# Hybrid RWKV / attention step on one core: norms by head in every row, attention queries left unnormalized

## The chip, the cores and the metric

The kernel runs on one core of one Trainium2 chip. The metric is the device time of one execution in microseconds (us); lower is better.

## The reference, cut to what matters

One layer over 1024 prompt tokens and 64 sample tokens, D = 1024, all in float32: RMS norm, one input projection, three token mixers in parallel (RWKV-7 with 8 heads of 64, sliding-window attention with 8 query and 2 key heads of 64, cross-attention with 4 heads of 128 into 256 memory tokens), gates, output projection, then a convolutional feed-forward part. The four norms by head are what the change touches:

```
kk = kk / max(sqrt(sum(kk * kk over 64)), 1e-12)                  # RWKV key, 8 heads
o = (o - mean) * rsqrt(var + GN_EPS) * ln_g + ln_b                # RWKV output, 8 heads
q = rms(q, swa_qn_g); k = rms(k, swa_kn_g)                        # window attention, 8 + 2 heads
qm = rms(qm, mem_qn_g)                                            # cross-attention, 4 heads
s = q.k * 64**-0.5 - slope * dist;  s = qm.mk * 128**-0.5         # scores, then softmax
```

## The kernel before, in words

Activations lie with channels on the 128 partitions and tokens along the free dimension. Tokens go in three groups g = 0, 1, 2 of T = 384, 384 and 320. For each group there is a `mix_block` (projections, mixers) and an `ffn_block`.

Every engine runs two threads, interleaved by one list written out ahead (`order`, used by `weave`). The *dense* thread is the projections: weights come in units of 128x512 by DMA (SP queue), ACT copies a unit to `w_hi` (L206), POOL subtracts to get `w_lo` (L215), PE makes 12 matmuls of it (L235 to L237). A ring of five units lets ACT and POOL run ahead of PE. An entry 0 of `order` is half a unit: six matmuls. A tile is two units; when it ends, DVE reads it out of one of two accumulators (L1560 for `pr` tiles with the token shift L1539 to L1551 behind it, L1567 for gates), and PE can't start the tile after next before that. The *chain* thread is the mixers; an entry 1 is one step of it on every engine. Each engine executes its queue strictly in order, so a chain instruction that waits also holds up the dense work behind it.

In `mix_block` the chain has four parts:

- `prep`, 14 steps, one behind each of the RWKV tiles 2 to 13, then two more with half a tile of dense work between them. Step 9 sums the squares of `kk`, steps 10 to 13 make the inverse root, step 13 ends with the operands ready (`rp_done`).
- `scan`, the chunks of 64 tokens, which begins with a wait for `rp_done`.
- `post`, 9 steps: mean, variance, inverse root, gain, bias, gate, split in `o_hi`, `o_lo`.
- `attn_prep`, 8 steps: squares of the nine tiles of `pa` (four of queries, one of keys, four of memory queries), sums, inverse root, product; then `attn`, items of 128 queries with scores, softmax, transposes, values.

After `prep` the steps are spread evenly over the 132 half units that are left: 101 steps in groups 0 and 1, 97 in group 2.

A norm by head was made "in rows": `to_rows` is a set of constant matrices that add the squares of every head into one row of a PSUM tile of T columns (one accumulating matmul for each tile of 128 channels), the inverse root is computed once on 128xT, and `from_rows` matrices copy each row back to the partitions of its head (one matmul a tile). The inverse root is Ln, then Exp on ACT (`rsqrt_act`), then a Newton step of three DVE instructions (`rsqrt`, L287, L289, L291). Each instruction waits for the one before.

Of the kernel before, what the change touches and what calls it, by code (L numbers as in the profile page):

```python
# [11 lines left out]
ALU = mybir.AluOpType  # L12
AX = mybir.AxisListType

P = 128
# [267 lines left out]

def rsqrt(dve, xs, t, y, sem, n):

    dve.wait_ge(sem, n + 2)
    dve.tensor_tensor(t, xs, y, ALU.mult).then_inc(sem, 1)  # L287
    dve.wait_ge(sem, n + 3)
    dve.scalar_tensor_tensor(t, t, -0.5, y, ALU.mult, ALU.mult).then_inc(sem, 1)  # L289
    dve.wait_ge(sem, n + 4)  # L290
    dve.scalar_tensor_tensor(y, t, 1.5, y, ALU.add, ALU.mult).then_inc(sem, 1)  # L291
# [8 lines left out]
def first_block(nc, c):  # L300
    a, T = c.a, GROUPS[0][1]
    with Phase(nc, "first") as f:
# [18 lines left out]
        def _(sp):  # L321
            def chain():
# [10 lines left out]
                for dst, src in ((c.ident, "ident"), (c.ones_head, "ones_head"), (c.lora, "lora"),  # L333
                                 (c.to_rows, "to_rows"), (c.from_rows, "from_rows")):
                    sp.dma_start(dst[...], a[src]).then_inc(c.consts_in, 16)
# [227 lines left out]
N_PREP, N_POST, N_ATTN_PREP = 14, 9, 8  # L563
# [4 lines left out]
def mix_block(nc, c, g):  # L568
# [18 lines left out]
    with Phase(nc, f"g{g}m") as f:  # L587
# [15 lines left out]
        def rooms(at):  # L603
# [12 lines left out]
        mask, xs, t, y = (give(TW) for _ in range(4))  # L616
# [16 lines left out]
        nsq, nxs, nt, ny = give(4, TW), give(TW), give(TW), give(TW)  # L633

        asq, axs, at_, ay = give(4, TW), give(TW), give(TW), give(TW)
# [16 lines left out]
            "mean centred squared var n_root spread post o_hi o_lo "  # L652
            "a_squared a_rows a_root a_spread a_done before cache "
# [16 lines left out]
        def _(pe):  # L670
            def keys():
# [11 lines left out]
                pe.wait_ge(c.consts_in, 16 * 5)  # L683
# [6 lines left out]
            def prep():  # L690
# [28 lines left out]
                yield  # L719
                yield  # L720
# [7 lines left out]
                pe.wait_ge(S["dstep"], 5)  # L728
                products(*((1 + m, c.ones_head[:, :], t3[:, m, 0:T]) for m in range(4)))
# [97 lines left out]
            def post():  # L827
# [7 lines left out]
                for m in range(4):  # L835
                    mm = pe.matmul(bank[4][:, 0:T], c.to_rows[:, m, :], nsq[:, m, 0:T], start=(m == 0), stop=(m == 3))
                mm.then_inc(S["var"], 1)
# [3 lines left out]
                pe.wait_ge(S["n_root"], ROOT)  # L841
                for m in range(4):
                    pe.wait_ge(S["centred"], 4)
                    pe.matmul(bank[m][:, 0:T], c.from_rows[:, m, :], ny[:, 0:T], start=True, stop=True).then_inc(S["spread"], 1)
# [3 lines left out]
                yield  # L848

            def attn_prep():  # L850
                yield
                for ns in (range(0, 4), range(4, 8), range(8, 9)):
                    for n in ns:
                        pe.wait_ge(S["a_squared"], n + 1)
                        pe.matmul(bank[5][:, 0:T], c.to_rows[:, n, :], asq[:, n % 4, 0:T], start=(n == 0),  # L855
                                  stop=(n == 8)).then_inc(S["a_rows"], 1)
                    yield
# [4 lines left out]
                for n in range(9):  # L862
                    if n >= 5:
                        pe.wait_ge(S["a_done"], n - 4)
# [1404 lines left out]
```

## Time and profile before

| | |
|---|---|
| median of 3 runs | 2249.27 us (2247.49 to 2250.12) |
| the profiled execution | 2246.76 us, its span 2244.9 us |
| PE busy | 2117.5 us, 94% of the span |
| DVE, ACT, POOL busy | 1121.6, 938.4, 1136.6 us |
| mean granted TensorE clock | 0.983 |

PE's busy time counts from the start of a matmul to its modelled end, and matmuls overlap; how long a row of them holds the engine is read from the starts. A float32 matmul shows as two records.

### The profile page before, as it was taken

To read this page: it belongs to the slowest core of one execution; us is meant where nothing else is said; L and a number is where in the kernel's file an instruction comes from. 1 tells how busy PE (TensorE), PEld (TensorE's weight loads), DVE (VectorE), ACT (ScalarE), POOL (GpSimd) and SP (SyncE) were. 2 spreads that over 40 slices of the span, in tenths; PEclk is the share of its full clock that TensorE was granted. 3 is DMA by queue.
4 is the path that set the end of the run, shared out by engine and by line. 5 is a ranking of instruction groups with operands and counts; after the bars stand their busy time and mean duration, and the time that the engine had idled before them with its cause. 6 is when DMAs were issued, how large, how long until landed. Compare 5 with 4: busy or idle time off the path is not lost. (4 is left out here: it accounts for less than half of the span.)

```text
span 2244.9 us, 42906 instructions
## 1 busy us (share of the span) xinstructions
PE 2117.5 (94%) x17042; PEld 1972.2 (88%) x17042; DVE 1121.6 (50%) x2048; ACT 938.4 (42%) x1888; POOL 1136.6 (51%) x933
## 2 busy tenths in 40 slices
PE   5989999899999998999998999999999989899998
PEld 4878887799999987888788999999889877799998
DVE  5673345455665237433554566632664255457740
ACT  4422335445444433232463444444432355355542
POOL 5543333365666654333334656665543333567775
PEclk8999999999999999999999999999999999999999
DMA  5421122363444433112225534444321333644453
GB/s 177 147 67 58 57 85 91 126 213 113 127 126 145 147 123 94 49 48 79 91 78 184 173 113 127 126 149 139 116 76 54 91 112 97 195 152 147 146 159 123
DMA packets 158150, 264.86 MB, mean 118 GB/s; under 512 B 20096, under 2 KB 53120, under 8 KB 157952
## 3 DMA queue, kind: packets, MB, share of 16 engines
q1 hardware_dynamic: 157376, 261.08, 37.2%
q8 instruction: 136, 2.23, 0.4%
q10 hardware_dynamic: 576, 1.05, 0.1%
q14 instruction: 62, 0.51, 0.1%
HBM read 242.60 MB, written 19.46 MB: 117 GB/s over the span
## 5 line engine op out<-in xcount | busy, mean ns | idle before, releaser
L215 POOL TENSOR_TENSOR k_w_lo<-k_raw,k_w_hi 128x512 fp32r<-128x512 f32 x832 | 1088.3, 1320 | 1016.7 <-ACT k_w_hi L206 972.6
L206 ACT ACTIVATE k_w_hi<-k_raw 128x512 fp32r<-128x512 f32 x832 | 500.0, 617 | 383.4 <-PE k_acc L237 129.3
L235 PE MATMUL k_acc<-k_x_hi,k_w_hi 128*128 128x384 f32 (+1 forms) x1152 | 416.6, 362 | 15.0 <-PEq L70 10.0
L237 PE MATMUL k_acc<-k_x_hi,k_w_lo 128*128 128x384 f32 (+1 forms) x1152 | 379.1, 329 | 0.0
L236 PE MATMUL k_acc<-k_x_lo,k_w_hi 128*128 128x384 f32 (+1 forms) x1152 | 378.6, 329 | 0.0
L235 PEld LDWEIGHTS k_acc<-k_x_hi,k_w_hi 128*128 128x128 f32 x1152 | 219.2, 190 | 54.3 <-issue 29.9
L236 PEld LDWEIGHTS k_acc<-k_x_lo,k_w_hi 128*128 128x128 f32 x1152 | 219.4, 190 | 5.6 <-issue 1.4
L237 PEld LDWEIGHTS k_acc<-k_x_hi,k_w_lo 128*128 128x128 f32 x1152 | 218.5, 190 | 0.0
L235 PE MATMUL k_acc<-k_o_hi,k_w_hi 128*128 128x384 f32 (+1 forms) x288 | 98.0, 340 | 24.4 <-POOL k_w_lo L215 9.7
L235 PE MATMUL k_acc<-g0f_xg_hi,k_w_hi 128*128 128x384 f32 x352 | 118.7, 337 | 2.2 <-DVE g0f_a_raw L1982 2.2
L235 PE MATMUL k_acc<-g1f_xg_hi,k_w_hi 128*128 128x384 f32 x352 | 118.7, 337 | 2.2 <-DVE g1f_a_raw L1982 2.2
L236 PE MATMUL k_acc<-g1f_xg_lo,k_w_hi 128*128 128x384 f32 x352 | 118.3, 336 | 0.0
L236 PE MATMUL k_acc<-g0f_xg_lo,k_w_hi 128*128 128x384 f32 x352 | 118.2, 336 | 0.0
L237 PE MATMUL k_acc<-g1f_xg_hi,k_w_lo 128*128 128x384 f32 x352 | 118.2, 336 | 0.0
L237 PE MATMUL k_acc<-g0f_xg_hi,k_w_lo 128*128 128x384 f32 x352 | 118.1, 336 | 0.0
L235 PE MATMUL k_acc<-g2f_xg_hi,k_w_hi 128*128 128x320 f32 x352 | 110.6, 314 | 2.4 <-DVE g2f_a_raw L1982 2.4
L236 PE MATMUL k_acc<-g2f_xg_lo,k_w_hi 128*128 128x320 f32 x352 | 109.4, 311 | 0.0
L237 PE MATMUL k_acc<-g2f_xg_hi,k_w_lo 128*128 128x320 f32 x352 | 109.4, 311 | 0.0
L236 PE MATMUL k_acc<-k_o_lo,k_w_hi 128*128 128x384 f32 (+1 forms) x288 | 96.5, 335 | 0.0
L237 PE MATMUL k_acc<-k_o_hi,k_w_lo 128*128 128x384 f32 (+1 forms) x288 | 96.3, 335 | 0.0
L235 PEld LDWEIGHTS k_acc<-k_o_hi,k_w_hi 128*128 128x128 f32 x288 | 55.7, 193 | 30.0 <-POOL k_w_lo L215 20.3
L737 PEld LDWEIGHTS g0m_bank<-g0m_room 64*64 64x64 f32 x1728 | 64.7, 134 | 10.1 <-issue 9.1
(710 smaller groups left out, 4476.6 us busy)
## 6 DMA issues: line engine op xcount, KB each, us to landing
k_raw<-w_up SPq DMA_DIRECT2D x264, 256.0 KB, 2.8
k_raw<-w_gate SPq DMA_DIRECT2D x144, 256.0 KB, 3.1
k_raw<-w_down SPq DMA_DIRECT2D x96, 256.0 KB, 3.8
k_raw<-w_rwkv SPq DMA_DIRECT2D x84, 256.0 KB, 3.0
k_raw<-w_branch SPq DMA_DIRECT2D x72, 256.0 KB, 3.5
k_raw<-w_attn SPq DMA_DIRECT2D x60, 256.0 KB, 2.9
k_raw<-w_out SPq DMA_DIRECT2D x48, 256.0 KB, 3.0
k_raw<-w_down_end SPq DMA_DIRECT2D x24, 256.0 KB, 3.4
```

Of the source, the lines that this page charges most:

```text
L206: act.activation(c.w_hi[s][:, 0:n], c.raw[s][:, 0:n], ACT.Copy).then_inc(c.hi_done, 1)
L215: pool.tensor_tensor(c.w_lo[s][:, 0:n], c.raw[s][:, 0:n], c.w_hi[s][:, 0:n].bitcast(F32), ALU.subtract).then_inc(c.lo_done, 1)
L235: pe.matmul(out, wh, xh, start=(u.begins and k == 0), stop=False)
L236: pe.matmul(out, wh, xl, start=False, stop=False)
L237: mm = pe.matmul(out, wl, xh, start=False, stop=(u.ends and k == u.kt - 1))
L737: mm = pe.matmul(out[h, j, :], lhs[h, j, :], rhs[h, j, :], start=(k == 0), stop=(k == len(operands) - 1))
```

## The change

1. `prep`: the four `to_rows` matmuls of step 9 become four with `ones_head` (a matrix that adds over the 64 partitions of a head and gives the sum to all of them), each into a bank of its own. DVE reads four banks. The inverse root is made on 128x4T; the Newton instructions go to step 11 (one) and 12 (two). The four `from_rows` matmuls go; one DVE product over 128x4T takes the place of four from PSUM. The bonus sums (four matmuls) move from step 13 to step 11. `B` is computed last.
2. `post`: the same, with 11 steps; the Newton instructions, 128x4T each, stand in steps 6, 7 and 8, gain and bias together in step 9.
3. `attn_prep`: nine squares into nine tiles. One matmul for the keys' sums (128xT), then eight with 32 columns of `ones_head` or `ones` into the four quarters of the partitions of two banks: the sums of the query heads. ACT copies these, PE turns them (two transposes an item), DVE reads 12 numbers for each query, and ACT and DVE make inverse roots `qf` of 128x36. The nine `from_rows` matmuls and eight of the nine products are gone. The keys are normalized as before and multiplied by the query gain on ACT into `kq`.
4. `attn`: `qf` stands in place of the constant 0.125 where the scores are read (four instructions of 256 columns a step for two of 512) and as the scale of the memory's Exp. The memory keys are multiplied by `mqn` once (`c.mk` in group 0, `cmk` in group 2).
5. 1.2 MB less of constants are loaded; the mix phase has four semaphores more (six new, two gone).

```diff
@@ prep, PE
-                pe.wait_ge(S["tan"], 2 + 7)
+                pe.wait_ge(S["tan"], 2 + 8)
+                pe.wait_ge(S["g_done"], 2)
                 pe.wait_ge(S["sq_done"], 1)
                 for m in range(4):
-                    mm = pe.matmul(bank[0][:, 0:T], c.to_rows[:, m, :], sq[:, m, 0:T], start=(m == 0), stop=(m == 3))
-                mm.then_inc(S["rows"], 1)
-                yield
-                yield
-                yield
-                pe.wait_ge(S["p_root"], ROOT)
-                pe.wait_ge(S["g_done"], 4)
-                products(*((b, c.from_rows[:, m, :], y[:, 0:T]) for m, b in ((0, 5), (1, 0))))
-                yield
-                pe.wait_ge(S["got"], 2)
-                products(*((b, c.from_rows[:, m, :], y[:, 0:T]) for m, b in ((2, 5), (3, 0))))
-                pe.wait_ge(S["tan"], 10)
+                    pe.matmul(bank[m][:, 0:T], c.ones_head[:, :], sq[:, m, 0:T], start=True, stop=True).then_inc(S["rows"], 1)
+                yield
+                yield
+                pe.wait_ge(S["p_root"], 1)
                 pe.wait_ge(S["dstep"], 5)
-                products(*((1 + m, c.ones_head[:, :], t3[:, m, 0:T]) for m in range(4)))
+                products(*((m, c.ones_head[:, :], t3[:, m, 0:T]) for m in range(4)))
@@ prep, DVE
+                for m in range(4):
+                    dve.wait_ge(S["rows"], m + 1)
+                    ins = dve.tensor_scalar(xs[:, m, 0:T], bank[m][:, 0:T], 1e-24, None, ALU.max)
+                ins.then_inc(S["p_root"], 1)
+                yield
+                yield
+                root = (xs[:, :, 0:T], t[:, :, 0:T], y[:, :, 0:T], S["p_root"], 1)
+                newton(dve, 0, *root)
+                yield
+                newton(dve, 1, *root)
+                newton(dve, 2, *root)
+                yield
+                dve.wait_ge(S["p_root"], ROOT)
+                dve.tensor_tensor(ar[:, X_KK, 0:T], ar[:, X_KK, 0:T], y[:, :, 0:T], ALU.mult).then_inc(S["got"], 1)
+                dve.wait_ge(S["mixed"], 14)
+                for m in range(4):
+                    dve.wait_ge(S["prod"], 12 + m + 1)
+                    dve.tensor_tensor(ar[:, X_BONUS.start + m, 0:T], bank[m][:, 0:T], ar[:, X_V.start + m, 0:T], ALU.mult)
+                dve.wait_ge(S["got"], 1)
+                dve.tensor_tensor(ar[:, X_B, 0:T], ar[:, X_KK, 0:T], t2[:, :, 0:T], ALU.mult).then_inc(S["rp_done"], 1)
@@ post, DVE
+                for k in range(3):
+                    yield
+                    newton(dve, k, nxs[:, :, 0:T], nt[:, :, 0:T], ny[:, :, 0:T], S["n_root"], 1)
+                yield
+                dve.wait_ge(S["n_root"], ROOT)
+                for m in range(4):
+                    dve.scalar_tensor_tensor(o[:, m, 0:T], o[:, m, 0:T], vec(c, "ln_g", m), ny[:, m, 0:T], ALU.mult,
                                              ALU.mult).then_inc(S["post"], 1)
@@ attn_prep, PE
+                pe.wait_ge(S["a_squared"], 9)
+                pe.matmul(bank[5][:, 0:T], c.ones_head[:, :], asq[:, 4, 0:T], start=True, stop=True).then_inc(S["a_rows"], 1)
+                pe.wait_ge(S["n_root"], 1)
+                for j in range(4):
+                    rows = slice(32 * j, 32 * j + 32)
+                    pe.matmul(bank[4][rows, 0:T], c.ones_head[:, 0:P:4], asq[:, j, 0:T], start=True, stop=True)
+                for j in range(4):
+                    rows = slice(32 * j, 32 * j + 32)
+                    mm = pe.matmul(bank[0][rows, 0:T], c.ones[:, 0:32], asq[:, 5 + j, 0:T], start=True, stop=True)
+                mm.then_inc(S["q_rows"], 1)
+                yield
+                yield
+                pe.wait_ge(S["q_read"], 1)
+                for n, b in enumerate((4, 0)):
+                    for p, it in enumerate(items):
+                        mm = pe.transpose(bank[b][0:it.nq, p * P:(p + 1) * P], q_rows[:, n, it.q0:it.q0 + it.nq], c.ident[:, :])
+                mm.then_inc(S["q_turned"], 1)
@@ attn, ACT
+                act.activation(kq[:, k_all], kw[:, k_all], ACT.Identity, scale=vec(c, "qn")).then_inc(S["kq"], 1)
@@ attn, DVE
+                    for jj in range(2):
+                        i, col = 4 * e + 2 * half + jj, 2 * (2 * half + jj) + e
+                        ins = dve.scalar_tensor_tensor(
+                            s[p % 2][0:it.nq, i, 0:nk], bank[2 * half + e][0:it.nq, jj * 256:jj * 256 + nk],
+                            qf[0:it.nq, p, col:col + 1], c.alibi[0:it.nq, i, it.first:2 * P], ALU.mult, ALU.add)
```

## Rows read from the trace of the kernel before

**Rows 1.** The page, busy time of each engine

```profile
PE 2117.5 (94%) x17042; PEld 1972.2 (88%) x17042; DVE 1121.6 (50%) x2048; ACT 938.4 (42%) x1888; POOL 1136.6 (51%) x933
```

**Rows 2.** Waits of PE over the span: us in total, times, longest

```profile
PE g2m_bank L688 <- DVE g2m_room L291: 4.9, 1, 4.9
PE g1m_bank L688 <- DVE g1m_room L291: 4.4, 1, 4.4
...
PE g1m_bank L865 <- DVE g1m_room L291: 2.6, 1, 2.6
```

**Rows 3.** Timeline of PE, end of `prep` in group 1: start, us, instruction

```profile
872.64 2.82 PE L716 MATMUL g1m_bank<-g1m_room,k_to_rows 128*128 128x384 f32 x8 [2.79 <-ACT g1m_room L998]
881.15 0.41 PE L235 MATMUL k_acc<-k_x_hi,k_w_hi 128*128 128x384 f32 x1 [1.53 <-DVE g1m_ar L1560]
894.15 2.93 PE L688 MATMUL g1m_bank<-g1m_room,k_from_rows 128*128 128x384 f32 x4 [4.41 <-DVE g1m_room L291]
908.43 1.92 PE L737 MATMUL g1m_bank<-g1m_room 64*64 64x128 f32 x32
```

**Rows 4.** Timeline of DVE, the same stretch

```profile
882.30 0.55 DVE L1234 TENSOR_SCALAR g1m_room<-g1m_bank 128x384 f32<-128x384 f32 x1
...
886.21 1.43 DVE L1539 TENSOR_TENSOR g1m_ar<-g1m_ar 128x383 f32<-128x383 f32 x1
...
890.36 1.61 DVE L287 TENSOR_TENSOR g1m_room<-g1m_room 128x384 f32<-128x384 f32 x1
...
901.92 1.76 DVE L1247 TENSOR_TENSOR g1m_ar<-g1m_ar,g1m_room 128x1536 f32<-128x1536 f32 x1
903.60 1.94 DVE L1250 TENSOR_TENSOR g1m_ar<-g1m_bank,g1m_ar 128x384 f32<-128x384 f32 x4
```

**Rows 5.** Timeline of POOL, the same stretch

```profile
884.66 8.43 POOL L215 TENSOR_TENSOR k_w_lo<-k_raw,k_w_hi 128x512 fp32r<-128x512 f32 x6 [4.54 <-ACT k_w_hi L206]
900.74 1.27 POOL L215 TENSOR_TENSOR k_w_lo<-k_raw,k_w_hi 128x512 fp32r<-128x512 f32 x1 [7.64 <-ACT k_w_hi L206]
```

**Rows 6.** Timeline of ACT, the same stretch

```profile
871.01 1.48 ACT L998 ACTIVATE g1m_room<-g1m_ar 128x1536 f32<-128x1536 f32 x1 [7.94 <-DVE g1m_ar L1218]
...
882.88 0.53 ACT L278 ACTIVATE g1m_room<-g1m_room 128x384 f32<-128x384 f32 x1 [7.01 <-DVE g1m_room L1234]
```

**Rows 7.** A stretch of 4 us, columns as its head says

```profile
core 0: us, PE busy (x) PEld busy (x) DVE busy (x) ACT busy (x) POOL busy (x), PEclk, DMA share, GB/s
894.00:898.00 4.00, 3.85 (x8) 2.64 (x9) 2.90 (x8) 0.00 (x0) 0.00 (x0) 0.50 0.22 66
```

**Rows 8.** Groups of PE instructions by shape, group 1: busy, mean ns

```profile
L929 PE MATMUL g1m_bank<-k_ident,g1m_room 128*128 128x128 f32 x24 | 3.1, 272 | 0.0
```

**Rows 9.** Timeline of PE, `post` to `attn` in group 1

```profile
1066.60 2.74 PE L831 MATMUL g1m_bank<-g1m_o,k_ones_head 128*128 128x384 f32 x8
...
1115.87 1.13 PE L878 MATMUL g1m_bank<-g1m_kw,g1m_pa 64*128 64x256 f32 x8
...
1130.53 3.54 PE L921 MATMUL g1m_bank<-k_ident,g1m_room 128*128 128x128 f32 x16 [1.99 <-DVE g1m_room L1469]
...
1142.76 1.94 PE L942 MATMUL g1m_bank<-g1m_room 128*64 128x512 f32 x8
```

**Rows 10.** Timeline of DVE, `post` in group 1

```profile
1084.14 3.23 DVE L1379 SCALAR_TENSOR_TENSOR g1m_o<-g1m_o,k_vecs,g1m_ar 128x384 f32<-128x384 f32 x4
...
1117.05 1.29 DVE L1432 SCALAR_TENSOR_TENSOR g1m_room<-g1m_bank,k_alibi 128x512 f32<-128x512 f32 x2 [0.52 <-PE g1m_bank L878]
```

**Rows 11.** Timeline of ACT, last steps of `post`, last square of `attn_prep`, group 1

```profile
1087.87 1.93 ACT L1077 ACTIVATE k_o_hi<-g1m_o 128x384 fp32r<-128x384 f32 x4 [2.56 <-DVE g1m_o L1384]
...
1094.84 0.52 ACT L1085 ACTIVATE g1m_room<-g1m_pa 128x384 f32<-128x384 f32 x1 [0.28 <-PE g1m_bank L855]
```

**Rows 12.** Timeline of POOL where group 0's mix phase ends

```profile
446.16 1.26 POOL L215 TENSOR_TENSOR k_w_lo<-k_raw,k_w_hi 128x512 fp32r<-128x512 f32 x1 [9.38 <-issue]
```

More of the change, by code:

```diff
@@ L332, in chain @@
                 yield
-                for dst, src in ((c.ident, "ident"), (c.ones_head, "ones_head"), (c.lora, "lora"),
-                                 (c.to_rows, "to_rows"), (c.from_rows, "from_rows")):
+                for dst, src in ((c.ident, "ident"), (c.ones_head, "ones_head"), (c.lora, "lora")):
                     sp.dma_start(dst[...], a[src]).then_inc(c.consts_in, 16)
@@ L615, in mix_block @@
         t1, t2, t3, sq = (give(4, TW) for _ in range(4))
-        mask, xs, t, y = (give(TW) for _ in range(4))
+        mask, xs = give(TW), give(4, TW)
+        t, y = sq, t1
         half, one_ka = give(8), give(4)
@@ L632, in mix_block @@
         give = rooms(0)
-        nsq, nxs, nt, ny = give(4, TW), give(TW), give(TW), give(TW)
-        asq, axs, at_, ay = give(4, TW), give(TW), give(TW), give(TW)
+        nsq, nxs, ny = give(4, TW), ar[:, X_R, :], ar[:, X_V, :]
+        nt = nsq
+        give = rooms(0)
+        asq, axs, at_, ay = give(9, TW), give(TW), give(TW), give(TW)
+        q_rows = asq[:, 0:2, :]
+        kq = give(5 * P)
+        qxs, qt, qf = (give(3, 12) for _ in range(3))
         s = [give(8, 2 * P)]
@@ L651, in mix_block @@
             "t2 t2_read t3 t3_read s0p xs xs_read sa sa_read ssum state osum o_read "
-            "mean centred squared var n_root spread post o_hi o_lo "
-            "a_squared a_rows a_root a_spread a_done before cache "
+            "mean centred squared var n_root post o_hi o_lo "
+            "a_squared a_rows a_root q_rows q_read q_turned q_root a_done kq gained before cache "
             "v_turned v_tok scores biased topped sunk shifted exps summed inverse scaled turned pt_read pv "
@@ L835, in post, with attn_prep @@
                 for m in range(4):
-                    mm = pe.matmul(bank[4][:, 0:T], c.to_rows[:, m, :], nsq[:, m, 0:T], start=(m == 0), stop=(m == 3))
-                mm.then_inc(S["var"], 1)
+                    pe.matmul(bank[m][:, 0:T], c.ones_head[:, :], nsq[:, m, 0:T], start=True, stop=True).then_inc(S["var"], 1)
+                for _ in range(9):
+                    yield
+            def attn_prep():
                 yield
@@ L847, in post @@
                 yield
-                yield
-            def attn_prep():
-                yield
[L852 to L856, printed above, removed]
-                    yield
-                yield
-                yield
-                pe.wait_ge(S["a_root"], ROOT)
-                pe.wait_ge(S["post"], 4)
-                for n in range(9):
-                    if n >= 5:
-                        pe.wait_ge(S["a_done"], n - 4)
-                    pe.matmul(bank[n % 5][:, 0:T], c.from_rows[:, n, :], ay[:, 0:T], start=True,
-                              stop=True).then_inc(S["a_spread"], 1)
-                    if n in (4, 8):
-                        yield
             def scores(p, half):
@@ L884, in m_scores @@
                 keys = c.mk if it.own else cmk
+                if g == 0 and p == 0 or not it.own:
+                    pe.wait_ge(S["gained"], 1)
                 if p >= 1:
@@ L1071, in post @@
                 yield
-                rsqrt_act(act, c, nxs[:, 0:T], nt[:, 0:T], ny[:, 0:T], S["n_root"], 1)
-                for _ in range(5):
+                rsqrt_act(act, c, nxs[:, :, 0:T], nt[:, :, 0:T], ny[:, :, 0:T], S["n_root"], 1)
+                for _ in range(7):
                     yield
@@ L1082, in attn_prep @@
                 for n in range(9):
[L1083 to L1085 removed]
+                    act.activation(asq[:, n, 0:T], pa[:, n, 0:T], ACT.Square).then_inc(S["a_squared"], 1)
                     if n in (3, 7):
@@ L1109, in m_exps @@
                     ins = act.activation(pm[0:it.nq, h, :], bank[4 + h // 2][0:it.nq, (h % 2) * 256:(h % 2 + 1) * 256],
-                                         ACT.Exp, bias=mneg[0:it.nq, h:h + 1], scale=float(P) ** -0.5,
+                                         ACT.Exp, bias=mneg[0:it.nq, h:h + 1], scale=qf[0:it.nq, p, 8 + h:9 + h],
                                          accum_out=mtotal[0:it.nq, h:h + 1])
```

136 lines of the change are left out of this document (68 added, 68 removed).

## The prediction, made before the changed kernel was run

> **What bounds the kernel now.** I read the page first: PE is busy 94% of the span, the others about half of it [rows 1]. So PE's work is the time, plus the places where its queue stands still. The list of PE's waits comes next. The long ones inside a mix phase are the norms: the `from_rows` matmuls wait 4.4 and 4.9 us in `prep` and 2.6 us in `attn_prep` for the last Newton instruction [rows 2]. Then the timelines of one group, to see why, since PE runs a fixed order and a chain step that is late stops the dense work too. Group 1's `prep` shows it: PE stands 2.79 us before L716, 1.53 us for an accumulator that DVE hasn't emptied, and 4.41 us before `from_rows` at 894.15 [rows 3]. In those 4.41 us DVE wasn't idle. A 383-column product took 1.43 us and the first Newton instruction, 384 columns, 1.61 us [rows 4], while POOL made six `w_lo` in one piece, 8.43 us from 884.66 [rows 5]. An uncontended DVE instruction over 1536 columns takes 1.76 us, 0.46 us for 384 [rows 4]. So a DVE instruction with two SBUF inputs waits about 1.1 us for POOL's while POOL has a backlog.
>
> The Trainium skill has a rule for this (SBUF — State Buffer, "SBUF: two separate sides"): DVE with two SBUF inputs and GpSimd take one shared port pair in turns, exclusively, for a whole instruction. The trace agrees, 1.43 and 1.61 us for instructions of about 0.5 [rows 4].
>
> **Part 1, PE's work.** Four 384-column matmuls hold PE some 2.6 us (2.74 us less the tail under the next [rows 9]), 0.65 each. A group loses 17 `from_rows` matmuls, and eight of its `to_rows` matmuls become narrow ones: 25 x 0.65 = 16.2 us. The narrow ones have 32 columns each in quarters of their own. The trace has halves: four 512-column matmuls of 64 columns took 1.94 us [rows 9], where 0.65 x 512 / 384 x 4 is 3.5, so two run at once. Eight quarters cost 1.3 us (four at once) to 5.2 us (none), I take 2.0, between four and two at once. Six transposes, 0.26 us each (12 in 3.1 us [rows 8]): 1.6 us. Net -12.6 us, for T = 320 about -10.4: **-35.6 us** in all. This arrives only if PE doesn't stand longer.
>
> The Trainium skill (TensorEngine Tiling, "Tiling Modes") says that four 128x32 tiles work in parallel and that a change of tiling drains the engine. By that alone the eight cost 1.3 us plus a drain, and the sum would be about 2 us lower over the three groups. No row here shows quarters.
>
> **Part 2, prep.** What decides is when DVE has `rp_done`, because the scan waits for it. In group 1, on before's clock:
> - Nothing changes up to 882.30, where DVE now reads four banks, 1.9 us instead of 0.5 (L1234 and L1250 give 0.55 and 1.94 for four [rows 4]): done 884.2.
> - Ln and Exp over 1536 take 1.4 to 1.5 us each (the Square over 1536 took 1.48 [rows 6]): done 887.2, where before, at 0.53 each from 882.88 [rows 6], they were over by 884.0. ACT holds its weight units so long, and POOL's backlog starts at about 887.9 instead of 884.66 [rows 5].
> - PE: tile 12 from 881.15, 8 half units in the 8.59 us to 889.74 [rows 3], so 1.05 each; bonus sums at 885.4 (2.6 us); tile 13 until 892.1; then six half units until 898.4, and it is at the scan.
> - DVE: tile 13 read and shifted (1.9 us), from 892.4; Newton 2 and 3, product, `B`: four at 1.7; bonus four in 1.94 [rows 4]. Together 10.6: 903.0 if POOL never interferes. POOL has five units to make after 892.2 (six in one piece and one later [rows 5], now all after 887.9). If each costs DVE 1.1 us: 908. I take 907, since the timeline shows strict alternation under a backlog.
> - From `rp_done` to the first gram matmul lie ACT's decays and five DVE instructions. Before, `rp_done` was 905.5 (end of L1250 [rows 4]) and the gram's matmuls began at 908.43 [rows 3], with 0.5 us to spare: 2.4 us. After: 909.4, against 908.43. So the 5.2 us of PE work and the 4.41 us wait are gone, and one wait of 8.6 to 11 us at the scan has come: **+1.0 us** (bounds -3.1 to +2.2).
> - The clock. After the 4.41 us wait the granted clock was 0.50 over 894 to 898 [rows 7], the lower level, 1.2 GHz, while PE worked. That price is inside before's 908.43. The new wait puts as long a stretch behind the gram, inside the scan: some 4 us at half rate, **+2.0 us** (0 to 3).
>
> Sum for `prep`: +3.0 us a group.
>
> **Part 3, post and attn_prep.** Step k after `prep` stands behind half unit 132k/103, rounded up, instead of 132k/101 (in groups 0 and 1). `post`, step 52, so comes behind half unit 67 instead of 68: on group 1's clock before, 1065.55 instead of 1066.60 [rows 9]. Variance sums end 1073.8, the four reads by DVE 1074.6, Ln and Exp 1077.5. From there DVE is full: three Newton instructions 5.0, a gate tile 0.5, gain, bias and gate 12 x 0.52 = 6.3: 11.8 us. Five POOL units fall into it; before, one cost the four bias instructions 1.1 us (3.23 instead of 2.1 [rows 10]). With 4.5 us for them the gates end at 1094 (1089.5 to 1095). Before, `o_hi`, one behind each gate product, ended at 1089.8 [rows 11], now 1094.5. Behind `o_hi` on ACT lie nine squares, two weight units and a gate's Tanh: before 5.6 us (1094.84 + 0.52 [rows 11]), after 5.2, as they no longer wait for sums: 1099.7. DVE has then also left the gate tile of half unit 80 unread, so PE stands at half unit 84 from 1088.4 on, for 5 us, then 5 us more in step 4 of `attn_prep`. Sums 0.65 + 2.0: 1102.3. Three half units and 1.7 us for a stretch at half clock: 1107.1. Transposes 1.6, five half units 5.2, values' transposes 0.5: first scores at 1114.4. `kq` is ready for it: `qf`, then DVE's nine small or 384-wide instructions and ACT's `kq` end about 4.5 us behind the transposes, PE comes 5.7 behind. Before, 1115.87 [rows 9]: -1.5 us. From there on, latency rules until L921, where PE waits 1.99 us for DVE at the same half unit as before, so the half unit in hand is given back in that wait. The score reads cost 4 x 0.34 instead of 1.29 [rows 10], +0.1 us each. Sum: **-1.3 us** a group (bounds -5.9, without POOL's interference, and +4.0, with quarters that don't overlap and `kq` 2 us late).
>
> **Part 4, small ones.** POOL stands 9.38 us at the end of a mix phase [rows 12] while it clears its 106 semaphores, 0.09 each; four more are 0.35 us, and PE waits there for the next `w_lo`: +1.0 us in three. The gain on `c.mk`, `cmk` (under 1 us on DVE) lies in PE's waits. The constants: 0, as nobody waits for them.
>
> **Sum.** 3 x (3.0 - 1.3) + 1.0 = +6, less 1 because groups at T = 320 have shorter instructions: +5 on the profiled execution's 2246.76, 2251.8. The runs' median is 2.5 us above that execution: **2254 us**. So the 35.6 us of PE work come back as waits of DVE's longer row, plus clock.
>
> **Rivals.**
> - *A, POOL and DVE don't meet much.* If ACT's delay lets POOL fill the ring in PE's waits, DVE's lists go uncontended: -3.1 + 2.0 in `prep`, -5.9 behind, +1: 3 x -7.0 + 1 = -20, 2229 us. For it: POOL works only half the time [rows 1]. Against: it met DVE in every such stretch [rows 4, 5].
> - *B, the waits go and nothing takes their place.* -35.6 and some 25 us of waits at the norms (4.4 and 2.6 [rows 2] and their like): 2190 us. It needs DVE to be ready 9 us earlier than my list; only speaks for it that PE is the bound [rows 1].
> - *C, worse: quarters don't overlap,* 5.2 instead of 2.0, 3.2 us in each group directly in the row from squares to scores, +10: 2264 us; with POOL's full price in both lists 2270. Decides from 4 us for eight.
> - *D, half of A:* 2241 us.
>
> **How the numbers follow.** Forecast, with its own range of 2249 to 2259: 0.48; A 0.14; B 0.04; C 0.16; D 0.18. Predicted 2254 us. The range reaches from A to C's end, 2228 to 2270, and leaves out B and some of the edges. A measurement tells about 0.2%, 4.5 us. Faster: A, B and D, 0.36. Slower: C and half of the forecast, 0.40. The same: the other half, 0.24.
>
> **What would show it.** In the changed profile: no PE wait before `from_rows`, but one of 8 to 11 us at the head of the scan, with Newton instructions of 1.7 to 2.9 us on DVE; a low granted clock just behind it; a wait for DVE's gate tile and for ACT's squares before the first sums of `attn_prep`; eight narrow matmuls in about 2 us; first scores 50 us behind `post`. If DVE's wide Newton instructions come at 1.7 us each, or PE arrives at the scan with `rp_done` there, the forecast is wrong and A or B holds.

## The result, and the profile after

The changed kernel takes 2267.52 us (median of 4 runs, 2266.26 to 2271.13), the kernel before 2249.69 in the same comparison (2247.49 to 2251.02): a ratio of 1.0080, 95% interval 1.0066 to 1.0094. The prediction was 2254 in a range of 2228 to 2270. The profiled execution took 2266.89 us, 20.1 more than the one of before, where the sum of the steps said 5.

The page of the changed kernel, busy time of each engine, to be held against [rows 1]:

```profile
PE 2097.0 (93%) x16958; PEld 1959.9 (87%) x16958; DVE 1157.7 (51%) x2089; ACT 955.3 (42%) x1903; POOL 1153.0 (51%) x933
```

PE has 84 matmul records less and 20.5 us less to do, and not the 35.6 that were taken from it: its mean granted clock fell from 0.983 to 0.968. There are two levels, 1 and 0.5 of full speed, so the share of the span at 0.5 is 2 x (1 - the mean): some 76 us before and 145 now.

Where the time went is read best from the starts of five matmuls in each group: the first one of `prep`, the first of the gram, of `post`'s means and of the scores, and the last one of the memory values in `attn`. The last stage ends at the first own matmul of the ffn phase. Sums over the three groups, in us, difference to before (222.5, 448.2, 144.6, 227.7, 290.2), with all kernels that were run:

```
                 prep>gram  gram>post  post>scores  scores>values  values>ffn    sum
changed            +5.4       +6.7        -2.1         +12.3          -2.2      +20.1
forecast           +3.0       +2.9        -1.4          +0.6           0         +5
only_prep          +5.2       +5.9        +1.8          -1.8          -0.8      +10.3
only_post          -0.3       -1.0       +24.4          +5.6          +0.4      +29.1
only_attn          +1.1       -0.1       -14.8          +5.0          +2.2       -6.6
filler             +5.4       +5.7        -1.0         +10.0          -2.1      +18.0
light_pool         -8.8       +5.2        -9.8          +8.7          +0.3       -4.4
no_newton          -7.6       +4.2       -10.4          +8.4          +1.6       -3.8
plain_scores       +5.8       +5.8        -0.8          +6.5          +0.8      +18.1
both              -17.9       +3.3       -15.3         +10.1          +1.9      -17.9
attn_bonus         -6.0       +3.2       -11.8          +4.9          -1.4      -11.1
attn_nn            -9.6       +3.3       -17.0          +3.5          -1.6      -21.4
only_attn again    +0.5        0.0       -10.7          +4.5          -2.7       -8.4
attn_bonus again   -7.1       +1.7       -13.4          +5.3          -1.1      -14.6
```

Each row is one execution, read to 0.1 us. Two kernels have a second profile (the last two rows), and the same kernel differs from itself by up to 4.1 and 4.9 us in one stage, so a difference of a few us in one stage alone is not to be read as the kernel's.

The waits of PE in the changed kernel (us in total, times, longest), in place of [rows 2]:

```profile
PE g1m_bank L750 <- DVE g1m_ar L1274: 8.2, 1, 8.2
...
PE k_acc L235 <- DVE g1m_gt L1611: 5.2, 1, 5.2
...
PE g1m_bank L851 <- ACT g1m_room L1092: 2.9, 1, 2.9
```

No wait stands before a `from_rows` matmul any more. In its place stand 8.2 us at the head of the scan (L750) and, behind `post`, 5.2 us for a gate tile and 2.9 for the squares; the other groups have the same within 1.1 us. Now group 1's `prep`, the timeline of PE, as [rows 3]:

```profile
881.06 2.82 PE L728 MATMUL g1m_bank<-g1m_room,k_ones_head 128*128 128x384 f32 x8 [2.80 <-ACT g1m_room L1007]
...
889.58 0.41 PE L235 MATMUL k_acc<-k_x_hi,k_w_hi 128*128 128x384 f32 x1 [1.53 <-DVE g1m_ar L1604]
...
916.04 1.12 PE L750 MATMUL g1m_bank<-k_ident,g1m_ar 64*64 64x64 f32 x16 [8.22 <-DVE g1m_ar L1274]
918.43 1.97 PE L743 MATMUL g1m_bank<-g1m_room 64*64 64x128 f32 x16 [1.27 <-DVE g1m_room L1311]
```

and what DVE did in it, as [rows 4]:

```profile
896.27 1.75 DVE L288 TENSOR_TENSOR g1m_room<-g1m_room 128x1536 f32<-128x1536 f32 x1
...
906.04 2.84 DVE L290 SCALAR_TENSOR_TENSOR g1m_room<-g1m_room 128x1536 f32<-128x1536 f32 x1
908.91 1.76 DVE L292 SCALAR_TENSOR_TENSOR g1m_room<-g1m_room 128x1536 f32<-128x1536 f32 x1
...
914.24 1.75 DVE L1274 TENSOR_TENSOR g1m_ar<-g1m_ar,g1m_room 128x1536 f32<-128x1536 f32 x1
```

with POOL in one piece beside it, as [rows 5]:

```profile
896.40 10.86 POOL L215 TENSOR_TENSOR k_w_lo<-k_raw,k_w_hi 128x512 fp32r<-128x512 f32 x7 [7.85 <-ACT k_w_hi L206]
```

Read together: ACT's long Ln and Exp move POOL's backlog behind them, to 896.40 to 907.26. The second Newton instruction lies in it and takes 2.84 us, the third and the products lie behind it and take 1.75 each. PE has nothing to do for the 8.22 us before 916.04. What follows is read from windows (columns as the head says):

```profile
core 0: us, PE busy (x) PEld busy (x) DVE busy (x) ACT busy (x) POOL busy (x), PEclk, DMA share, GB/s
907.00:911.00 4.00, 0.82 (x5) 0.50 (x3) 3.93 (x3) 0.00 (x0) 0.26 (x1) 0.99 0.42 127
911.00:925.00 14.00, 7.69 (x73) 6.74 (x74) 10.47 (x23) 2.12 (x6) 2.12 (x4) 0.52 0.00 1
925.00:939.00 14.00, 13.57 (x240) 12.08 (x238) 5.25 (x14) 4.15 (x9) 5.56 (x7) 1.00 0.19 57
```

PE's last work before the wait ends at 907.8. By 911 the clock is at its lower level, where it stays for nearly 14 us, and PE works in some 7.2 of them (7.69 in the window, which ends a little later). In groups 0 and 2 the low stretches at this place are 13.7 and 10.2 us long, with PE at work in 7.1 and 5.1.

The same for `post` to `attn` of group 1, PE as in [rows 9]:

```profile
1079.05 2.74 PE L837 MATMUL g1m_bank<-g1m_o,k_ones_head 128*128 128x384 f32 x8
...
1107.27 0.66 PE L235 MATMUL k_acc<-k_x_hi,k_w_hi 128*128 128x384 f32 x1 [5.17 <-DVE g1m_gt L1611]
...
1112.43 1.65 PE L851 MATMUL g1m_bank<-g1m_room,k_ones_head 128*128 128x384 f32 x2 [2.90 <-ACT g1m_room L1092]
1114.01 1.51 PE L856 MATMUL g1m_bank<-g1m_room,k_ones_head 128*32 128x384 f32 x8
1115.30 1.01 PE L859 MATMUL g1m_bank<-g1m_room,k_ones 128*32 128x384 f32 x8
...
1127.93 1.14 PE L880 MATMUL g1m_bank<-g1m_room,g1m_pa 64*128 64x256 f32 x8 [1.98 <-ACT g1m_room L1135]
...
1130.94 2.01 PE L880 MATMUL g1m_bank<-g1m_room,g1m_pa 64*128 64x256 f32 x8
...
1145.60 2.95 PE L930 MATMUL g1m_bank<-k_ident,g1m_room 128*128 128x128 f32 x16 [4.46 <-DVE g1m_room L1509]
```

and DVE:

```profile
1091.19 1.76 DVE L288 TENSOR_TENSOR g1m_room<-g1m_ar 128x1536 f32<-128x1536 f32 x1 [0.97 <-ACT g1m_ar L280]
1092.98 2.74 DVE L290 SCALAR_TENSOR_TENSOR g1m_room<-g1m_room,g1m_ar 128x1536 f32<-128x1536 f32 x1
...
1096.11 2.37 DVE L292 SCALAR_TENSOR_TENSOR g1m_ar<-g1m_room,g1m_ar 128x1536 f32<-128x1536 f32 x1
1098.52 4.15 DVE L1399 SCALAR_TENSOR_TENSOR g1m_o<-g1m_o,k_vecs,g1m_ar 128x384 f32<-128x384 f32 x4
...
1129.18 1.66 DVE L1471 SCALAR_TENSOR_TENSOR g1m_room<-g1m_bank,g1m_room,k_alibi 128x256 f32<-128x256 f32 x4 [1.29 <-PE g1m_bank L880]
...
1142.11 3.43 DVE L1509 TENSOR_TENSOR g1m_room<-g1m_room 128x1024 f32<-128x1024 f32 x2
```

with POOL's `w_lo` beside the last one:

```profile
1142.23 2.22 POOL L215 TENSOR_TENSOR k_w_lo<-k_raw,k_w_hi 128x512 fp32r<-128x512 f32 x1 [9.75 <-ACT k_w_hi L206]
```

In the kernel before, the second scores, the same DVE instruction (L1469 there) and POOL beside it:

```profile
1118.19 1.13 PE L878 MATMUL g1m_bank<-g1m_kw,g1m_pa 64*128 64x256 f32 x8
1128.12 2.36 DVE L1469 TENSOR_TENSOR g1m_room<-g1m_room 128x1024 f32<-128x1024 f32 x2
1130.05 3.77 POOL L215 TENSOR_TENSOR k_w_lo<-k_raw,k_w_hi 128x512 fp32r<-128x512 f32 x2 [11.08 <-ACT k_w_hi L206]
```

Up to the first scores all is about as forecast (48.88 us behind L837). Behind them 3.0 us are lost before the turning of the weights (L930): 17.67 us, where it was 14.66 before [rows 9]. Three rows add up to it. The second scores come 3.01 behind the first, not 2.32 (1118.19 in the kernel before), and take 2.01 at the lower clock, not 1.13: 1.5 with what stands between them. The score read takes 1.66, not 1.29 [rows 10]: 0.4. L1509 takes 3.43, where the same instruction of before took 2.36, since a `w_lo` now starts with it: 1.1.

### The profile page after: what moved, and what is told of

Its sections match the earlier page's. It is cut to its first block and busy times, and to the rows that moved or that the text cites. A ratio compares the mean times of both kernels' runs of the same rounds, so it can differ in the third digit from the quotient of the medians.

```text
span 2264.7 us, 42796 instructions
## 1 busy us (share of the span) xinstructions
PE 2097.0 (93%) x16958; PEld 1959.9 (87%) x16958; DVE 1157.7 (51%) x2089; ACT 955.3 (42%) x1903; POOL 1153.0 (51%) x933
## 3 DMA queue, kind: packets, MB, share of 16 engines
q10 hardware_dynamic: 576, 1.05, 0.1%
## 5 line engine op out<-in xcount | busy, mean ns | idle before, releaser
L215 POOL TENSOR_TENSOR k_w_lo<-k_raw,k_w_hi 128x512 fp32r<-128x512 f32 x832 | 1103.6, 1338 | 1021.7 <-ACT k_w_hi L206 976.8
L743 PEld LDWEIGHTS g1m_bank<-g1m_room 64*64 64x64 f32 x1728 | 66.3, 136 | 12.1 <-issue 9.9
```

The source lines that it names most:

```text
L215: pool.tensor_tensor(c.w_lo[s][:, 0:n], c.raw[s][:, 0:n], c.w_hi[s][:, 0:n].bitcast(F32), ALU.subtract).then_inc(c.lo_done, 1)
L743: mm = pe.matmul(out[h, j, :], lhs[h, j, :], rhs[h, j, :], start=(k == 0), stop=(k == len(operands) - 1))
```

## The experiments

Theory: DVE's row of 1536-column instructions, lengthened by POOL's `w_lo`, sets the head of the scan and the end of `post`; the PE work that is saved becomes a wait, and the wait costs clock. Rivals: the row is long without POOL; the attention part, or the clock alone, makes the loss. The first four runs took the change apart, the next four took terms out of it, the last took two out together and tried versions. The kernel before, measured beside the first four, the next four and the rest, took 2247.71, 2249.45 and 2246.95 us.

**only_prep.** Part 1 of the diff on the kernel before.

```diff
-                    mm = pe.matmul(bank[0][:, 0:T], c.to_rows[:, m, :], sq[:, m, 0:T], start=(m == 0), stop=(m == 3))
+                    pe.matmul(bank[m][:, 0:T], c.ones_head[:, :], sq[:, m, 0:T], start=True, stop=True).then_inc(S["rows"], 1)
...
+                newton(dve, 1, *root)
+                newton(dve, 2, *root)
```

> The kernel before with part 1 (prep) alone. My theory: DVE's row of 128x1536 instructions sets when the scan may begin, PE waits some 8 us at the scan's head in each group, and the long low clock behind that wait costs PE 3 to 4 us more: +5 us a group, ratio 1.006 to 1.008 (about +15 us). Rival 1, the clock costs next to nothing and only the later start of the scan counts: +1.5 us a group, +5 us, ratio 1.002. Rival 2, prep is not to blame and the slowdown is in post and attention: PE's 2.6 us a group less are a gain, -8 us, ratio 0.997.

Measured: 2259.27 us (2257.34 to 2265.63), 1.0054 (1.0032 to 1.0077). The wait at the scan (L746 there) is 8.2 to 8.3 us in each group, as in the whole change, and so are the two stages in the table, +5.2 and +5.9. That is 11.6 us more than before, under the 15 that were expected and well over rival 1's 5. What the change loses in `prep` and in the scan is part 1's alone.

**only_post.** Part 2 alone, with the attention's old norm behind it.

```diff
-N_PREP, N_POST, N_ATTN_PREP = 14, 9, 8
+N_PREP, N_POST, N_ATTN_PREP = 14, 11, 8
...
-                    pe.matmul(bank[m][:, 0:T], c.from_rows[:, m, :], ny[:, 0:T], start=True, stop=True).then_inc(S["spread"], 1)
```

> The kernel before with part 2 (post) alone. My theory: DVE is full from the inverse root to the gate products, o_hi comes 5 us later, the squares of attn_prep with it, PE stands before the sums: +4 to +6 us a group, +12 to +18 us, ratio 1.005 to 1.008. Rival: the wait for the wide Newton instructions only replaces the wait for from_rows, and PE's 2.6 us a group less come through: -8 us, ratio 0.9965.

Measured: 2273.38 us (2270.56 to 2275.29), 1.0116 (1.0093 to 1.0139). Some 25 us more than before, above what was expected. The timeline of PE and its waits:

```profile
1105.24 5.04 PE L852 MATMUL g1m_bank<-g1m_room,k_to_rows 128*128 128x384 f32 x8 [7.54 <-ACT g1m_room L1082]
...
1123.11 5.19 PE L862 MATMUL g1m_bank<-g1m_room,k_from_rows 128*128 128x384 f32 x10 [3.34 <-DVE g1m_room L292]
```

The squares come 7.5 us late, and the old norm's eighteen matmuls stand behind them, the first of each kind at the lower clock: `post` to the scores is 24.4 us longer in the three groups. In the whole change part 3 has removed these matmuls, and the stage is 2.1 us shorter than before. The delay still has a price there, about half of that: only_attn, without it, has -14.8.

**only_attn.** Parts 3 and 4 alone: sums in quarters, `qf` in the score reads.

```diff
+                    pe.matmul(bank[4][rows, 0:T], c.ones_head[:, 0:P:4], asq[:, j, 0:T], start=True, stop=True)
...
+                            qf[0:it.nq, p, col:col + 1], c.alibi[0:it.nq, i, it.first:2 * P], ALU.mult, ALU.add)
```

> The kernel before with parts 3 and 4 (attn_prep, attn) alone. My theory: this part is the good one. PE loses 7 us of matmuls a group, DVE loses eight products and gains nothing wide; o_hi comes as early as before, so first scores come 6 to 8 us sooner; score reads and clock take 1 to 3 us back: -4 to -6 us a group, -12 to -18 us, ratio 0.992 to 0.995. Rival: the new row squares, sums, copies, transposes, root, kq is as long as the old one, and the score reads cost 3 to 5 us a group: +5 to +10 us, ratio 1.002 to 1.005.

Measured: 2238.23 us (2233.02 to 2242.33), 0.9957 (0.9944 to 0.9971). Faster than both kernels, by 9.5 us against the one before, where 12 to 18 were expected: the first scores come 4.8, 7.1 and 2.9 us sooner in the three groups, and not 6 to 8. The quarters at full clock:

```profile
1093.45 0.88 PE L864 MATMUL g1m_bank<-g1m_room,k_ones_head 128*32 128x384 f32 x8
1094.15 0.83 PE L867 MATMUL g1m_bank<-g1m_room,k_ones 128*32 128x384 f32 x8
```

Each row is four matmuls; the second four start 0.70 us behind the first, about the 0.65 of one 384-column matmul, and the dense work stands 1.46 us behind the first. The Trainium skill (TensorEngine Tiling, "Tiling Modes") has four such tiles in parallel: the trace agrees, eight take 1.5 us. Rival C of the prediction is out.

The parts' differences are +11.6, +25.7 and -9.5 us, +27.8 together, where the whole has +18. They don't add, and the table shows where: from `post` to the scores they have +1.8, +24.4 and -14.8, +11.4 together, and the whole has -2.1. The late squares cost 24.4 where the old norm follows them, and some 11 to 13 where part 3 has taken it away (from only_attn's -14.8 to -2.1, with prep's +1.8 in it).

**filler.** The changed kernel with eight matmuls more, of 384 columns, in step 14 of `prep`, where PE waits.

```diff
+                for _ in range(8):
+                    pe.matmul(bank[5][:, 0:T], c.ident[:, :], c.lora[:, 1, 0:T], start=True, stop=True)
```

> The changed kernel with eight matmuls of 128x384 in float32 more on PE in step 14 of prep (5.2 us a group, constants into a bank that nothing reads). They lie in the 8.2 us wait at the scan's head. If the clock behind that wait costs PE 3 to 4 us a group (theory), the work keeps the clock up and the kernel gets faster by 6 to 12 us against the changed kernel (2256 to 2262 us), though PE does 15.6 us more. If the clock's price is small or comes back in later waits (rival), the time stays at 2267 within 3 us.

Measured: 2266.73 us (2261.20 to 2270.29), 1.0085 (1.0057 to 1.0114), the same as without them. The rival's time came, not the theory's. The wait at the scan fell from 8.2 to 3.0 us and the end did not move: some 5 us of matmuls a group cost nothing there, which shows that the head of the scan is DVE's. The lower clock came anyway, a little later, as the windows show:

```profile
905.00:911.00 6.00, 4.83 (x21) 3.45 (x19) 5.93 (x7) 0.00 (x0) 0.00 (x0) 1.00 0.14 47
911.00:915.00 4.00, 0.68 (x16) 0.54 (x16) 3.58 (x8) 2.12 (x6) 0.14 (x2) 0.90 0.00 0
915.00:925.00 10.00, 9.75 (x102) 8.56 (x104) 5.16 (x17) 0.38 (x1) 2.91 (x4) 0.70 0.09 28
```

The low stretches became shorter, 6.8 us in each group for 13.7, 13.7 and 10.2, but they lie where PE works: in 15.7 us of them in all, for 19.4. That is 1.9 us at half rate, and the stage behind is +5.7 instead of +6.7, less than two executions of one kernel differ. So the run did not take the low clock away, and says nothing certain on its price.

**light_pool.** The changed kernel, POOL's work taken from beside the two rows.

```diff
+    n = 32 if light else n
...
+                    pool_unit(pool, c, u.index + SPLIT, light=27 <= r < 34 or 68 <= r < 76)
```

> The changed kernel, in which POOL makes only 32 of the 512 columns of w_lo for the weight units 27 to 33 and 68 to 75 of each mix phase (the rest of these low parts is left as it was). Those are the units that fall beside DVE's rows in prep and post. Theory: what DVE loses to POOL there is lost by the kernel: five units at some 0.75 in prep (3.7 us) and five in post (3.8 us), so DVE's 2.84 at 128x1536 becomes 1.76, the wait at the head of the scan falls from 8.2 to about 4.5, and the time from 2267 to about 2245. Rival: the row is long by itself and POOL's backlog only moves; then about 2264, with the scan's wait at 7 or more.

Measured: 2241.02 us (2237.88 to 2246.04), 0.9961 (0.9943 to 0.9980), 26 us below the changed kernel (22 were expected). DVE's row and the wait:

```profile
891.70 1.75 DVE L291 SCALAR_TENSOR_TENSOR g1m_room<-g1m_room 128x1536 f32<-128x1536 f32 x1
893.49 1.76 DVE L293 SCALAR_TENSOR_TENSOR g1m_room<-g1m_room 128x1536 f32<-128x1536 f32 x1
...
1080.56 2.26 DVE L1400 SCALAR_TENSOR_TENSOR g1m_o<-g1m_o,k_vecs,g1m_ar 128x384 f32<-128x384 f32 x4
```

```profile
PE g1m_bank L751 <- DVE g1m_ar L1275: 4.6, 1, 4.6
```

Where POOL is nearly silent, 2.84 becomes 1.75 and 4.15 becomes 2.26, and the wait 4.6, as expected. The Trainium skill (SBUF — State Buffer, "SBUF: two separate sides") has DVE with two SBUF inputs and GpSimd take turns for whole instructions; the trace agrees, a POOL instruction of 32 columns costs DVE almost nothing, one of 512 cost the second Newton instruction 1.1 us. The rival (2264, a wait of 7 or more) falls.

The same kernel takes apart what is lost behind the first scores, as its second scores come at full clock. PE in group 1:

```profile
1109.18 1.13 PE L881 MATMUL g1m_bank<-g1m_room,g1m_pa 64*128 64x256 f32 x8 [1.98 <-ACT g1m_room L1136]
...
1111.52 1.13 PE L881 MATMUL g1m_bank<-g1m_room,g1m_pa 64*128 64x256 f32 x8
...
1125.29 3.54 PE L931 MATMUL g1m_bank<-k_ident,g1m_room 128*128 128x128 f32 x16 [4.46 <-DVE g1m_room L1510]
```

The turning is 16.11 us behind the first scores, 1.45 more than before: the 0.4 of the read and the 1.1 that its L1510 (3.43 us again) loses to POOL, without any of the clock's 1.5. PE waited the same 1.98 us ahead of the first scores as in the changed kernel, so this gap alone doesn't bring the lower clock.

Other traces on record have the terms in other pairs. The clock's shows purely in only_attn, whose kernel was profiled twice:

```profile
1106.36 1.13 PE L888 MATMUL g1m_bank<-g1m_room,g1m_pa 64*128 64x256 f32 x8 [1.74 <-ACT g1m_room L1143]
...
1109.26 2.08 PE L888 MATMUL g1m_bank<-g1m_room,g1m_pa 64*128 64x256 f32 x8
...
1122.91 1.97 PE L938 MATMUL g1m_bank<-k_ident,g1m_room 128*128 128x128 f32 x16 [2.34 <-DVE g1m_room L1514]
```

```profile
1106.93 1.13 PE L888 MATMUL g1m_bank<-g1m_room,g1m_pa 64*128 64x256 f32 x8 [1.75 <-ACT g1m_room L1143]
...
1109.24 1.14 PE L888 MATMUL g1m_bank<-g1m_room,g1m_pa 64*128 64x256 f32 x8
...
1121.95 1.97 PE L938 MATMUL g1m_bank<-k_ident,g1m_room 128*128 128x128 f32 x16 [2.35 <-DVE g1m_room L1514]
```

The turning stands 16.55 us behind the first scores in one execution and 15.02 in the other: 1.5 us for the lower clock, which came in one and not in the other behind the same waits. The second is 0.36 more than before, the new reads alone. only_post, with the old reads at full clock and the order of the changed kernel, has 15.72 and an L1468 of 3.43 us: 1.1 for POOL alone. So each of the three terms of this item stands by itself.

**no_newton.** The changed kernel without Newton's instructions in `prep` and `post`.

```diff
-                newton(dve, 0, *root)
-                newton(dve, 1, *root)
-                newton(dve, 2, *root)
-                dve.wait_ge(S["p_root"], ROOT)
+                dve.wait_ge(S["p_root"], 3)
```

> The changed kernel without Newton's instructions in prep (three) and post (three): the roots are left as ScalarE's Ln and Exp give them. Theory: DVE's row from the roots sets both ends. It gets shorter by 1.75 + 2.84 in prep (the first lies in a wait for the last tile) and by 1.76 + 2.74 + 2.37 in post, so the waits at the scan (8.2) and for the gate tile (5.2) fall to some 3.6 and 0: about 2235. Rival: the change's loss lies in the clock and in the attention part, and these waits only change places with others of PE: 2255 to 2262.

Measured: 2241.67 us (2240.14 to 2247.36), 0.9964 (0.9952 to 0.9976). 26 us below the changed kernel, where some 32 were expected. The wait at the scan is 3.4 to 4.5. The row loses 4.6 us there and the wait 4.8 in group 1, so the row sets it. Behind `post` less than the 6.9 us came back: the wait for the gate tile went from 5.2 to 2.0, that for ACT's squares stayed or grew, from 2.4 to 2.9 up to 2.9 to 3.9.

**both.** The two edits together.

> The changed kernel with both edits that were tried alone: no Newton's instructions in prep and post, and POOL's w_lo cut to 32 of 512 columns for the weight units 27 to 33 and 68 to 75 of each mix phase. Each alone came to 2241. Theory: both shorten the same row of DVE, and PE can only get back what it still waits for: 3.5 to 4.7 at the head of the scan and part of the 3.9 for ScalarE's squares, some 6 us a group: 2222. Rival 1: the two add up (26 each), 2215. Rival 2: the rows had ceased to be the limit already with one edit, PE's clock and the attention are: 2235 to 2241.

Measured: 2227.58 us (2220.29 to 2228.70), 0.9900 (0.9878 to 0.9923). 40 us below the changed kernel, between the theory's 45 and what one edit gives (26). The scan's head is nearly free, the squares are not:

```profile
894.51 0.68 PE L751 MATMUL g1m_bank<-k_ident,g1m_ar 64*64 64x64 f32 x16 [1.03 <-DVE g1m_ar L1272]
```

```profile
PE g1m_bank L852 <- ACT g1m_room L1093: 4.0, 1, 4.0
```

In the table `prep` is then 17.9 us shorter than before and `post` to the scores 15.3. This is not all PE work. Part 1 takes four matmuls a group, 7.4 us of PE in all; the waits before `from_rows`, 13.7 in the three groups, are gone as well, and 3.1 at the head and 5.0 before the gram have come, which is 5.6 less; the rest was not followed. Of the 28 us that parts 2 and 3 take from PE by the prediction's count, 15.3 arrive. The scan (+3.3) and the attention (+10.1) stay longer than before, so those losses have another cause than the length of the two rows.

**plain_scores.** The changed kernel with the old score reads.

```diff
-                            qf[0:it.nq, p, col:col + 1], c.alibi[0:it.nq, i, it.first:2 * P], ALU.mult, ALU.add)
+                        bank[2 * half + e][0:it.nq, :].rearrange("p (j k) -> p j k", j=2)[:, :, 0:nk], 0.125,
```

> The changed kernel with its score reads in the window attention as in the kernel before: two instructions of 512 columns with the constant 0.125 for four of 256 with a multiplier by row (so the norm of its queries is left out). Theory: DVE's reads (1.66 for two instead of 1.29 for one) cost 0.37 each, some four to eight a group on the path: -1 us a group, 2264. Rival: they are the whole of the attention's loss (3.0 from the first scores to the sums and 2.5 behind it): -5 us a group, 2252.

Measured: 2263.78 us (2260.59 to 2266.49), 1.0057 (1.0038 to 1.0076), 3.7 us less. The theory said 3, the rival 15, which is out; the intervals of the two ratios overlap, so that the reads cost something is likely and its size is not settled. In its profiled execution the stage from the scores on went from +12.3 to +6.5, so the reads are a third to a half of that stage's loss by these two readings; the rest is there without them.

**attn_bonus.** only_attn with the bonus sums ahead of `from_rows`.

```diff
+                products(*((1 + m, c.ones_head[:, :], t3[:, m, 0:T]) for m in range(4)))
+                yield
                 pe.wait_ge(S["p_root"], ROOT)
                 products(*((b, c.from_rows[:, m, :], y[:, 0:T]) for m, b in ((0, 5), (1, 0))))
```

> The kernel before with the attention parts of the change alone, in which prep's four matmuls of the bonus sums stand ahead of from_rows instead of two steps behind. Theory: they fill 2.6 of the 4.4 us for which PE waits there for DVE's third Newton instruction, and nothing later needs them where they stood: 2 us a group, 2230 to 2233 against 2238 without it. Rival: the row that sets the scan is DVE's, and the time only moves to the scan's head: 2237 to 2240.

> The same kernel as attn_bonus, in more rounds and beside only_attn on the same chip: theory, 4 us below only_attn (2.0 to 3.5 of it from prep in each group, less what the scan gives back); rival, the same time within 2 us.

> The same kernel as only_attn, in more rounds, as the partner of attn_bonus: 2238, 0.9957 of the kernel before.

Measured: 2237.07 us (2235.17 to 2240.63), 0.9939 (0.9916 to 0.9963), the rival's time and not the theory's 2230 to 2233; measured again 2234.16 (2227.56 to 2237.29), 0.9931 (0.9911 to 0.9951), beside 2236.76 (2234.93 to 2239.16), 0.9947 (0.9930 to 0.9965), for only_attn. 2.6 us better side by side, where 4 were expected, with intervals that overlap: a gain is likely, not settled. In both profiles `prep` gains 7 to 8 us over the three groups against only_attn and the scan gives back 3.3 and 1.7. DVE is ready when PE comes, but in group 1 the gram finds the lower clock:

```profile
899.70 0.68 PE L748 MATMUL g1m_bank<-k_ident,g1m_ar 64*64 64x64 f32 x16 [0.20 <-DVE g1m_ar L1279]
902.09 3.59 PE L741 MATMUL g1m_bank<-g1m_room 64*64 64x128 f32 x32 [1.71 <-DVE g1m_room L1318]
```

The same happens in group 0. In group 2, behind waits of 0.50 and 1.71 us, and in group 0 of the second execution the gram stays at full clock, and the scan gives back nothing.

**attn_nn.** attn_bonus without Newton's instructions at the narrow roots of `prep`, `post` and the attention's keys.

```diff
-                rsqrt(dve, xs[:, 0:T], t[:, 0:T], y[:, 0:T], S["p_root"], 1)
-                rsqrt(dve, nxs[:, 0:T], nt[:, 0:T], ny[:, 0:T], S["n_root"], 1)
-                rsqrt(dve, axs[:, 0:T], at_[:, 0:T], ay[:, 0:T], S["a_root"], 1)
```

> The kernel before with the attention parts alone and the bonus sums moved (attn_bonus), without Newton's three instructions at each of prep's, post's and the attention keys' narrow roots; the roots are left as ScalarE's Ln and Exp give them. Theory: at 384 columns they are 0.5 to 1.5 us each, 2 to 4 us in a row, and PE still waits 1 to 3 us at two places of a group: -3 us a group, 2228. Rival: behind these waits stand others of the same length (squares, o_hi): 2234 to 2238.

Measured: 2222.16 us (2218.41 to 2225.28), 0.9883 (0.9862 to 0.9903), the fastest of all, 12 us below attn_bonus measured beside it, where 6 to 9 were expected; why it is more was not followed. It leaves out a refinement of the roots. Of the kernels that compute all that the one before does, attn_bonus and only_attn are the fastest.

## Why the prediction was near and still 15 us short

Up to the first scores the mechanism held: the PE work came back as waits of a longer row on DVE, plus clock. The waits stand where they were forecast, and light_pool, no_newton and filler show the cause. That 2267.5 us lies in the range of 2228 to 2270 is luck all the same: it is far above the forecast's own 2249 to 2259, and the range reached so high for rival C, whose quarters overlap in the trace. Step by step:

- **PE's work.** Near, with one row misread. The 24 records of [rows 8] are 24 transposes, for a transpose shows as one record: 0.13 us each and not 0.26. Six hold PE 0.57 us in the changed profile (1119.48 to 1120.05), where 1.6 were taken, so the sum was some 3 us a kernel too small. The eight narrow matmuls take 1.5 us at full clock, not the 2.0 taken; at the lower level, where they stood, four take 1.29, so eight 2.6.
- **Prep.** +1.0 a group was forecast up to the gram. The stage has +5.4 in three groups, 1.8 each. The waits are 8.22 and 1.27 for 8.6 to 11. DVE lost one Newton instruction's 1.1 us and 2.6 in the last tile's short instructions (1.10, 1.25 and 1.53 us for 0.56, 0.15 and 0.61), about what light_pool gives back. (An uncontended instruction of 384 columns takes 0.55 us [rows 4], not the 0.46 of the prediction; that changes little.)
- **The clock: mis-sized.** "Some 4 us at half rate, +2.0 us" became nearly 14 us of half clock, some 7.2 of them with PE at work. The scan stage has +6.7, where -1.05 and +2.0 a group make +2.9: the clock's term there is some 3.3 a group instead of 2.0, above its bound of 3. The low stretches behind the three waits agree: PE works in 19.4 us of them, 9.7 at half rate, 3.2 a group. The estimate took the length of the low stretch from [rows 7], behind a wait of 4.41 us with dense matmuls after it. Here turns and gram matmuls follow, with a second gap of 1.27 us between them.
- **Post and attn_prep.** -0.45 a group from `post` to the scores was forecast, -0.7 is measured. The row of Newton and gates ended 27.6 us behind L837 (1106.65), the sum had 28.4. The gate tile's wait is 5.17 for 5; that for the squares 2.9 for 5, as the half unit between the two took 2.26 us at the lower clock and the row had ended 0.8 us earlier. One part was off: `kq` was to be ready 4.5 us behind the transposes, and was at 1127.79, 7.5 us behind them, so PE waited 1.98 us for it. The transposes' missing 1 us made up for half of that.
- **Behind the first scores: the step that failed.** "The half unit in hand is given back in that wait. The score reads cost [...] +0.1 us each" gave +0.6 for three groups; +12.3 is measured, 11.7 of the 15 us that are missing. Three things were left out or taken too small, and group 1's first item shows each with its size. The second scores fell at the lower clock: 1.5 us. What brings it there is not shown: light_pool has the same 1.98 us for `kq` ahead and full clock, and only_attn had both behind the same waits. The reads stand on the path, once in this item: 0.4 (plain_scores: 4 us of the median in all, 6 of its profile). And the dense work stands one half unit further in the order of the attention, twelve matmul records behind the turning instead of six, so that POOL's `w_lo` starts together with L1509 (1142.23 and 1142.11) and not near its end (1130.05 behind 1128.12): 1.1. light_pool has the last two without the first. Over all items, only_post, the order without the reads, has +5.6 in this stage, and only_attn, the reads without the order, +5.0 and +4.5; how much of each is the clock stays open.
- **Small ones.** POOL's idle time at the end of a mix phase went from 9.38 [rows 12] to 9.66 us, 0.28 for 0.35. The last stage is 2.2 us shorter, not longer; this was not followed further.

Rival A's premise, that POOL and DVE don't meet much, did not hold in the change: three of its wide instructions and the gains took 2.84, 2.74, 2.37 and 4.15 us for 1.75 and 2.1. light_pool makes it nearly true and gives 2241, not A's 2229. That both came to 2228 doesn't speak for A, as it leaves out the Newton instructions too.

## What to carry to other kernels

Work taken from the bound engine is worth only what the next row on its path allows: make that row's length, instruction by instruction, before the saving is counted, with the price of every instruction that meets another engine at SBUF. Trading four matmuls for four times the columns on DVE pays only where DVE isn't on the path; here the part that made DVE's tiles smaller (128x36 for the queries) won and the two that made them four times wider lost. And which part of a change makes the loss is learned by running the parts alone and together, as their costs don't add.

## What the runs showed of the hardware

- The lower clock can come behind short gaps too, and need not. The first gram matmuls take 1.92 us at full clock [rows 3]. They took 3.59 in group 1 of attn_bonus, where PE had stood only 0.20 and 1.71 us, with 16 matmul records of turning (0.68 us together) between, and 1.96 in group 2 behind 0.50 and 1.71. The same kernel (only_attn) had its second scores at the lower clock in one execution and at full clock in the other. Filling most of the longer gap (filler) made the low stretches shorter, and did not keep the clock up.
- Matmuls of 32 output columns in four quarters overlapped fully: 0.70 us for four of 384 columns at full clock, 1.29 at the lower.
- What DVE loses to POOL goes by the length of POOL's instruction: 0.5 to 1.1 us a meeting with 512 columns, almost nothing with 32, whatever DVE's own width: a 128x1 instruction took 1.25 us instead of 0.15, one of 128x1536 2.84 instead of 1.75.
